# Decode step kernel: a DRAM-to-DRAM copy issued later, and page loads in another order

## The chip, the cores and the metric

The program runs on one core of one Trainium2 chip. The time is device microseconds of one execution. Before the change three executions took 1007.67 (the median), 1008.3 and 1002.5 us.

## The reference, cut to what matters

One inference step of two trunk layers. Each layer normalises its input, multiplies it with one wide weight matrix (`h @ w_in`) and feeds three token mixers: a gated linear recurrence (HGRN2), a sparse attention whose keys are chosen by an indexer (top k), and an attention with compressed, selected and windowed keys. 256 prompt tokens are computed beside 8 decoding sequences, each of which has 1024 past tokens in 8 pages of 128 rows. Beside the outputs the step returns new state:

```python
rows = jnp.concatenate([flat(dk_h), dv, ik_h, flat(nck_h), ncv, flat(nsk_h), nsv], axis=-1)
full = rows if past_rows is None else jnp.concatenate([past_rows.astype(dt), rows], axis=1)
dots = jnp.einsum('bthd,bsd->bths', iqb, ik, ...) * IDX_DIM ** -0.5   # indexer keys of all past tokens
sel = lax.top_k(score, n_top)[1]
wfull = wrows if win_rows is None else jnp.concatenate([win_rows.astype(dt), wrows], axis=1)
return y, rows, wfull[:, -min(WINDOW, lw):], s_new.astype(dt)
```

The third output, for the decoding sequences, is the window state: 511 old rows of each sequence and one new one. The 511 old rows are copied as they are.

## The kernel before, in words

All engines run their own instruction list; they meet at semaphores. Everything is float32. TensorE (PE) sets the order: for each layer it runs projections (L876, weights in 1 MB "slabs"), indexer scores (`key_scores`, L943), the recurrence (L1002 to L1087), prompt attention (L1098 to L1132), the compression of prompt tokens (L1145 to L1192), the page stage of the decoding sequences (L1200 to L1231), decode softmax and values (L1249 to L1311), branch products (L1328) and the output projection (L1336). Between dependent steps it runs pieces of independent projections (`mix`, L992), so that it need not wait.

**Slabs.** `STREAM` is the list of weight slabs in the order of use. There are three slots in SBUF (`NSLOT = 3`); SyncE (SP) loads each slab with `send(name)` (L641), which first waits until the slab three places earlier in the list has been used. The gate slabs g00 to g21 are used in the recurrence, two jobs of 16 matmuls each; m00 to m23 hold the merge gates, two `mix` pieces each.

**Indexer and recurrence.** `key_scores(pair)` waits for indexer keys of a pair of sequences (64 pages of 32 KB per layer; those of even page number are issued by SP, those of odd number by GpSimd, POOL). VectorE (DVE) meanwhile picks the top keys of the prompt (`top_keys`, L1786), and then prepares the factors of the recurrence: step `m i` (L1966, L1967, mark `m 0` at L1968). TensorE's products of step i (L1020, mark `a i`) wait for `m i`; behind each stand two projection jobs at most. Ahead of them PE waits for `sidx_a "relu"` (ScalarE, L1473), runs L1007 (mark `flat`), and DVE merges the products (L1862). SP loads the recurrent state S (2 MB, L693) after `flat`.

**Old window rows.** POOL issues the copy `s_win <- state_win` (L768, 4088 KB read from and written to DRAM) right behind the new rows of the layer (L765, L766). Its landing is waited for at the very end only (L815).

**Page stage.** The 64 key pages are worked in 8 units `u`. `load_keys(u)` brings 8 key pages of 256 KB (128 x 512 float32), 4 on SP (even pages) and 4 on POOL (odd), 2.10 MB together, into one of four buffers `KB[u % 4]`. Units 4 to 7 wait until unit u - 4 has been used (`pg_p`). `load_values(s)` brings 8 value pages of 128 KB (128 x 256 float32), again half on SP and half on POOL, 1.05 MB together. `window_keys(p)` brings 0.52 MB on SP. Unit u on PE is `page_scores` (L1200), for odd u `window_scores` (L1208), `compress` (L1221), and `compressed` (L1229, L1231) behind even ones. PE waits for the keys just ahead of L1200 and for the window keys ahead of L1208. The buffer `KB[3]` lies on memory that the compression stage of the prompt still uses. That stage has the marks `s` (L1158), `t` (L1167), `o` (L1175), `nb` (ScalarE, L1577) and last `sums` (DVE, L2097), which releases unit 3's buffer. Values of all sequences are needed at L1299 only.

SP's and POOL's lists are quoted below: each issues in order, so that a wait in one holds up all that stands behind it.

Of the kernel before, what the change touches and what calls it, by code (L numbers as in the profile page):

```python
# [307 lines left out]
def hybrid_step(nc, x_cols, pages_kv, page_table, state_win, win_k, win_v, state_hgrn, weights, small_w, cmp_w1,  # L308
                const, gate_rows, y_cols, z_keys, z_vals, p_hgrn, s_win, s_hgrn):
    ctx = ExitStack()  # L310
    with ctx:
# [3 lines left out]
        def sem(name):  # L315
            return ctx.enter_context(nc.semaphore(name))
# [204 lines left out]
        hg_p = Steps("hg_p", ["a diag"] + [f"a {i}" for i in range(8)] + ["o", "kfT", "kd", "sfin", "qk", "od", "kv 0", "odT", "kv 1", "ss"])  # L521
# [3 lines left out]
        spill_out, back_in = sem("spill_out"), sem("back_in")  # L525
# [7 lines left out]
        cp_p = Steps("cp_p", ["h", "out", "s", "t", "o"] + [f"gb {c}" for c in range(3)])  # L533
        cp_v = Steps("cp_v", ["sum", "s", "n", "nb", "ev"] + [f"gb {c}" for c in range(3)]
                     + ["sums"])
        cp_a = Steps("cp_a", ["hb", "hid", "out", "e", "nb", "t", "ev"])
# [52 lines left out]
        def page_of(part, l, page):  # L589
            o, rows, cols = PAGE_PARTS[part]  # L590
            return pages_kv[bass.ds(l, 1), bass.ds(page, 1), o:o + rows * cols].rearrange("a b (p c) -> p (a b) c", p=rows)[:, 0]
# [6 lines left out]
                        engine.dma_start(ikT[halves[h], pair, i * PAGE:(i + 1) * PAGE], page_of("index", l, pages[2 * pair + h, i]))\  # L598
                            .then_inc(ik_in[pair][i % 2], 16)

        def load_keys(engine, l, u, odd, pages):

            if u >= 4:
                engine.wait_ge(pg_p.sem, pg_p(l, f"u {u - 4}"))
            for e in range(2):
                for k in (odd, 2 + odd):
                    engine.dma_start(KB[u % 4][:, e, k, :], page_of("keys", l, pages[u // 2 + NPAIR * e, 4 * (u % 2) + k])).then_inc(page_in[u % 4][odd], 16)  # L607

        def load_values(engine, l, s, odd, pages):

            for i in range(odd, NPG, 2):
                engine.dma_start(V[:, s, i, :, :].rearrange("p a c -> p (a c)"), page_of("vals", l, pages[s, i])).then_inc(v_in[odd], 16)  # L612

        def window_keys(engine, l, p):

            if p >= 2:
                engine.wait_ge(pg_p.sem, pg_p(l, f"u {2 * p - 3}"))
            for e in range(2):
                engine.dma_start(kws[p % 2][:, e, :], win_k[l, p + NPAIR * e]).then_inc(win_in[p % 2], 16)
# [11 lines left out]
        def _(sp):  # L631
# [6 lines left out]
            for l in range(DEPTH):  # L638
                l1 = bass.ds(l, 1)

                def send(name):  # L641
                    slot = SLOT_AT[name][0]
                    at_ = STREAM.index(name)
                    if l and at_ < NSLOT:

                        sp.wait_ge(ga_p.sem, ga_p(l - 1, LAST_USE[LAST_IN_SLOT[slot]]))
                    if at_ >= NSLOT:

                        old = STREAM[at_ - NSLOT]
                        if old in SLAB_OF:  # L650
                            sp.wait_ge(proj_ready, l * NJOB + LAST_JOB[old])
                        elif old[0] == "m":
                            sp.wait_ge(mx_p.sem, mx_p(l, LAST_USE[old]))
                        else:
                            sp.wait_ge(ga_p.sem, ga_p(l, LAST_USE[old]))
                    for i, (dst, src) in enumerate(slab_sources(name, l)):
                        if name == "iq0" and i < 2:
                            sp.dma_start(dst, src).then_inc(iq_in[i], 16)
                            if l == 0:
                                x_columns(2 * i + 1)  # L660
                            if l == 0 and i == 0:
                                x_columns(2)
                        else:
                            sp.dma_start(dst, src).then_inc(slab_in[slot], 16)

                for name in FRONT:
# [4 lines left out]
                    if l == 0 and name == "iq1":  # L672
                        sp.dma_start(cst[:, NFIRST:], const[:, NFIRST:]).then_inc(consts_in, 16)
                        sp.dma_start(pt[:, :], page_table.rearrange("(o a) b -> o (a b)", o=1)).then_inc(pages_in, 16)
                        pages = {}
# [40 lines left out]
                sp.wait_ge(cp_p.sem, cp_p(l, "s"))  # L716
                load_keys(sp, l, 2, 0, pages)
                load_values(sp, l, 1, 0, pages)
                sp.wait_ge(cp_v.sem, cp_v(l, "sums"))
                load_keys(sp, l, 3, 0, pages)  # L720
                load_values(sp, l, 2, 0, pages)
                for name in ("m21", "m22"):
                    send(name)
                for u in range(4, NUNIT):
                    load_keys(sp, l, u, 0, pages)
                    if u % 2:
                        window_keys(sp, l, u // 2)
                sp.wait_ge(pg_p.sem, pg_p(l, "u 4"))
                for s in (4, 5):
                    load_values(sp, l, s, 0, pages)  # L730
# [20 lines left out]
        def _(pool):  # L751
# [4 lines left out]
            pages = page_numbers(pool, 1)  # L756
            for l in range(DEPTH):
# [7 lines left out]
                pool.dma_start(z_keys[l], Z[:, Z_IK:Z_IW, :]).then_inc(rows_out, 16)  # L765
                pool.dma_start(z_vals[l], Z[:, Z_NWV:Z_NSV + 1, :]).then_inc(rows_out, 16)  # L766

                pool.dma_start(s_win[l1].rearrange("a s w c -> (a s) w c"),  # L768
                               state_win[l1, :, 1:WIN, :].rearrange("a s w c -> (a s) w c")).then_inc(win_out, 16)

# [23 lines left out]
                pool.wait_ge(cp_p.sem, cp_p(l, "s"))  # L794
                load_keys(pool, l, 2, 1, pages)
                load_values(pool, l, 1, 1, pages)
                pool.wait_ge(cp_v.sem, cp_v(l, "sums"))
                load_keys(pool, l, 3, 1, pages)
                pool.wait_ge(spill_out, l * 16 + 16)
                load_values(pool, l, 2, 1, pages)  # L800
                for u in range(4, NUNIT):
                    load_keys(pool, l, u, 1, pages)
                pool.wait_ge(pg_p.sem, pg_p(l, "u 4"))
# [1484 lines left out]
```

## Time and profile before

| | |
|---|---|
| runs (us) | 1002.5, 1007.67, 1008.3 |
| profiled execution | 1005.99 us, span 1004.3 us, mean granted clock 0.98 |
| PE busy | 956.5 us (95%) |
| DVE busy | 481.1 us (48%) |
| ACT busy | 303.3 us (30%) |
| POOL busy | 132.4 us (13%) |
| DMA | 188.96 MB, mean 188 GB/s |

All times within the execution are counted from the start of the span. Layer 0 lasts to about 505 us, layer 1 to the end, and each stage lies some 495 us later in the second layer. PE, DVE, ACT and POOL are the compute engines.
### The profile page before, as it was taken

The numbers are of one execution on the slowest core, as the hardware profiler recorded it, in microseconds if no ns is written. First come the engines' busy times: TensorE is split into PE (matmuls) and PEld (weight loads), VectorE is DVE, ScalarE is ACT, GpSimd is POOL, SyncE is SP. The second block draws the span as 40 slices with busy tenths as digits, with TensorE's granted clock in tenths as the row PEclk, the third lists the DMA queues.
The fourth block names the chain that finished last, engine by engine and source line by source line (L and its number), as shares of the span: only waits on it lengthen the run. The fifth ranks groups of instructions, "written<-read, shape, count | busy, mean of one in ns | idle before, by whom it ended". The sixth has DMA issues, their size and how long they took to land.

```text
span 1004.3 us, 16669 instructions
## 1 busy us (share of the span) xinstructions
PE 956.5 (95%) x6058; PEld 775.0 (77%) x6058; DVE 481.1 (48%) x1350; ACT 303.3 (30%) x657; POOL 132.4 (13%) x258
## 2 busy tenths in 40 slices
PE   8999989999999979999999999899999997989998
PEld 6888768877777767888888886688676866778887
DVE  4223588877746303124240345898785562041331
ACT  2135413237633112320111463222576311133000
POOL 0510000002031442000060000000020404500000
PEclk9999999999999989999999999999999999899999
DMA  7544635344197797334454446352443949952432
GB/s 256 200 170 153 211 152 210 106 156 169 42 314 264 289 379 255 136 126 136 158 175 139 151 138 261 141 197 85 148 158 100 374 168 380 374 190 87 161 133 86
DMA packets 56212, 188.96 MB, mean 188 GB/s; under 512 B 9154, under 2 KB 22850, under 8 KB 43586
## 3 DMA queue, kind: packets, MB, share of 16 engines
q1 hardware_dynamic: 42850, 138.56, 39.5%
q0 software_dynamic: 12992, 49.16, 12.9%
q8 instruction: 48, 0.79, 0.3%
q14 instruction: 34, 0.28, 0.1%
q10 hardware_dynamic: 288, 0.18, 0.1%
HBM read 177.47 MB, written 18.77 MB: 195 GB/s over the span
## 4 chain that ended last, share of the span: by engine, by line
PE 80%; DMA 7%; DVE 5%; ACT 3%; issue 2%; DVEq 2%; SPq 2%; ACTq 1%
PE ps L876 23%; PE ps L992 16%; PE ps L1328 9%; DMA arena<-in_pages_kv_dram 6%; PE ps L1336 6%; PE ps L1221 4%; PE ps L1020 3%; PE ps L865 2%; PE ps L1299 2%; PE ps L1132 2%; PE ps L1120 2%; PE ps L1100 1%; PE ps L1200 1%; PE ps L903 1%; PE ps L888 1%
## 5 line engine op out<-in xcount | busy, mean ns | idle before, releaser
L876 PE MATMUL ps<-hT,slab 128*128 128x264 f32 (+1 forms) x1184 | 272.8, 389 | 0.0
L876 PEld LDWEIGHTS ps<-hT,slab 128*128 128x128 f32 (+1 forms) x1184 | 224.4, 191 | 39.9 <-issue 2.1
L992 PE MATMUL ps<-hT,slab 128*128 128x264 f32 x768 | 182.9, 395 | 1.7 <-DVEq L2085 1.7
L992 PEld LDWEIGHTS ps<-hT,slab 128*128 128x128 f32 x768 | 145.6, 193 | 34.1 <-issue 3.3
L1348 ACT ACTIVATE arena<-ps 128x512 f32<-128x512 f32 (+21 forms) x152 | 69.7, 484 | 194.4 <-PE ps L876 70.1
L1328 PE MATMUL ps<-Y,slab 128*128 128x264 f32 x384 | 85.8, 386 | 0.0
L1328 PEld LDWEIGHTS ps<-Y,slab 128*128 128x128 f32 x384 | 73.0, 190 | 12.5
L1221 PEld LDWEIGHTS ps<-arena,w 128*128 128x128 f32 x512 | 61.1, 199 | 11.7 <-issue 10.0
L1221 PE MATMUL ps<-arena,w 128*128 128x128 f32 x512 | 64.1, 285 | 0.0
L1740 DVE SCALAR_TENSOR_TENSOR arena<-arena,small 128x264 f32<-128x264 f32 x26 | 11.0, 490 | 110.7 <-ACT arena L1423 110.7
L1336 PE MATMUL ps<-arena,slab 128*128 128x264 f32 x256 | 57.5, 387 | 2.3 <-DVEq L2225 2.3
L1336 PEld LDWEIGHTS ps<-arena,slab 128*128 128x128 f32 x256 | 48.5, 190 | 11.3 <-DVEq L2225 3.1
L598 POOL DMA_DIRECT2D arena<-in_pages_kv_dram x64 | 33.3, 520 | 160.6 <-DVEq L2241 122.5
L607 POOL DMA_DIRECT2D arena<-in_pages_kv_dram x64 | 35.0, 547 | 105.6 <-DVEq L2097 54.6
L2107 DVE TENSOR_TENSOR arena<-ps,arena 64x252 f32<-64x252 f32 x8 | 3.3, 412 | 90.0 <-ACT arena L1348 90.0
L1533 ACT ACTIVATE arena<-arena,st 128x128 f32<-128x128 f32 (+1 forms) x96 | 42.3, 443 | 8.1 <-DVEq L2010 7.1
L1486 ACT ACTIVATE arena<-ps 128x264 f32<-128x264 f32 x38 | 14.8, 389 | 80.5 <-PE ps L992 80.2
L612 POOL DMA_DIRECT2D arena<-in_pages_kv_dram x64 | 35.0, 546 | 29.2 <-PE ps L1221 26.7
L1348 ACT ACTIVATE Y<-ps 128x264 f32<-128x264 f32 x24 | 9.4, 390 | 87.0 <-PE ps L876 87.0
L1200 PE MATMUL ps<-arena,QC 128*32 128x512 f32 x128 | 18.8, 661 | 14.0 <-DMA arena<-in_pages_kv_dram 12.8
L888 PEld LDWEIGHTS ps<-slab,hT 128*128 128x128 f32 x128 | 25.2, 200 | 8.2 <-issue 4.7
L865 PE MATMUL ps<-arena,slab 128*128 128x264 f32 x128 | 30.2, 394 | 0.2 <-issue 0.2
(360 smaller groups left out, 1196.6 us busy)
## 6 DMA issues: line engine op xcount, KB each, us to landing
slab<-in_weights_dram SPq DMA_DIRECT2D x86, 1024.0 KB, 4.9
arena<-in_pages_kv_dram SPq DMA_DIRECT2D x64, 256.0 KB, 11.3
arena<-in_pages_kv_dram POOLq DMA_DIRECT2D x64, 256.0 KB, 8.2
arena<-in_pages_kv_dram POOLq DMA_DIRECT2D x64, 128.0 KB, 6.2
arena<-in_pages_kv_dram SPq DMA_DIRECT2D x64, 128.0 KB, 8.7
out_dram<-in_state_win_dram POOLq DMA_DIRECT2D x2, 4088.0 KB, 27.8
arena<-in_state_hgrn_dram SPq DMA_DIRECT2D x2, 2048.0 KB, 10.1
out_dram<-arena POOLq DMA_DIRECT2D x2, 2048.0 KB, 7.5
```

What stands on the lines that cost most here:

```text
L598: engine.dma_start(ikT[halves[h], pair, i * PAGE:(i + 1) * PAGE], page_of("index", l, pages[2 * pair + h, i]))\
L607: engine.dma_start(KB[u % 4][:, e, k, :], page_of("keys", l, pages[u // 2 + NPAIR * e, 4 * (u % 2) + k])).then_inc(page_in[u % 4][odd], 16)
L612: engine.dma_start(V[:, s, i, :, :].rearrange("p a c -> p (a c)"), page_of("vals", l, pages[s, i])).then_inc(v_in[odd], 16)
L865: last = mm(ps[:, n, 0:LT], stationary(name, job, k), XG[:, k, :], start=(k == 0), stop=(k == KD - 1))
L876: last = mm(ps[0:job[3], n % 2, 0:LT], v[:, k, job[2]:job[2] + job[3]], hT[:, k, :], start=(k == 0), stop=(k == KD - 1))
L888: last = mm(ps[:, n % 2, t * 256:t * 256 + width], hT[:, k, t * 128:t * 128 + 128], v[:, k, o:o + width], start=(k == 0), stop=(k == KD - 1))
L992: last = mm(ps[:, bank, 0:LT], v[:, k, (d % 2) * 128:(d % 2) * 128 + 128], hT[:, k, :], start=(k == 0), stop=(k == KD - 1))
L1221: last = mm(out[:, kv, :, 64 * hf:64 * hf + 64], w1[:, kv, t, :], blocks[:, :, o:o + 2 * NPB8], start=(t == 0), stop=(t == ST - 1))
L1328: last = mm(ps[:, d % 4, 0:LT], v[:, j, dd * 128:dd * 128 + 128], Y[:, a, j, :], start=(j == 0), stop=(j == 3))
L1336: last = mm(ps[:, d % 4, 0:LT], v[:, k, (d % 2) * 128:(d % 2) * 128 + 128], mT[:, k, :], start=(k == 0), stop=(k == KD - 1))
L1348: return A(out, in_, ACT.Copy, scale=scale)
L1533: A(x[:, j, :], x[:, j, :], ACT.Exp, scale=-1.0, bias=st[:, c + j:c + j + 1], accum_out=sa[:, c + j:c + j + 1])
```

## The change

Three edits, each in both layers. POOL waits for `a 0` of the recurrence before it issues the copy of old window rows. Unit 3's keys are loaded in two halves: sequence 0 of each pair after the mark `o`, sequence 1 after `sums`. The values of sequence 2 are issued after `nb`, ahead of the keys of unit 3, and slab m21 is sent between the halves; slab m22 is sent behind the last keys and window keys. POOL's wait for the spill transfer moves up with the values.

```diff
-        def load_keys(engine, l, u, odd, pages):
+        def load_keys(engine, l, u, odd, pages, sequences=(0, 1)):
...
-            for e in range(2):
+            for e in sequences:
...
                 sp.wait_ge(cp_p.sem, cp_p(l, "s"))
                 load_keys(sp, l, 2, 0, pages)
                 load_values(sp, l, 1, 0, pages)
+                sp.wait_ge(cp_a.sem, cp_a(l, "nb"))
+                load_values(sp, l, 2, 0, pages)
+                sp.wait_ge(cp_p.sem, cp_p(l, "o"))
+                load_keys(sp, l, 3, 0, pages, (0,))
+                send("m21")
                 sp.wait_ge(cp_v.sem, cp_v(l, "sums"))
-                load_keys(sp, l, 3, 0, pages)
-                load_values(sp, l, 2, 0, pages)
-                for name in ("m21", "m22"):
-                    send(name)
+                load_keys(sp, l, 3, 0, pages, (1,))
                 for u in range(4, NUNIT):
                     load_keys(sp, l, u, 0, pages)
                     if u % 2:
                         window_keys(sp, l, u // 2)
+                send("m22")
...
+                pool.wait_ge(hg_p.sem, hg_p(l, "a 0"))
                 pool.dma_start(s_win[l1].rearrange("a s w c -> (a s) w c"),
                                state_win[l1, :, 1:WIN, :].rearrange("a s w c -> (a s) w c")).then_inc(win_out, 16)
...
+                pool.wait_ge(spill_out, l * 16 + 16)
+                pool.wait_ge(cp_a.sem, cp_a(l, "nb"))
+                load_values(pool, l, 2, 1, pages)
+                pool.wait_ge(cp_p.sem, cp_p(l, "o"))
+                load_keys(pool, l, 3, 1, pages, (0,))
                 pool.wait_ge(cp_v.sem, cp_v(l, "sums"))
-                load_keys(pool, l, 3, 1, pages)
-                pool.wait_ge(spill_out, l * 16 + 16)
-                load_values(pool, l, 2, 1, pages)
+                load_keys(pool, l, 3, 1, pages, (1,))
```

## Rows read from the trace of the kernel before

**Rows 1.** Waits of PE: line, releaser, us in total, times, longest.
```profile
PE ps L1200 <- DMA arena<-in_pages_kv_dram: 12.8, 2, 7.3
PE ps L943 <- DMA arena<-in_pages_kv_dram: 6.8, 2, 4.1
```

**Rows 2.** Timeline of PE, page stage, layer 0: start, us, operation, [idle before].
```profile
347.83 1.06 PE L1200 MATMUL ps<-arena,QC 128*32 128x512 f32 x8
...
349.25 3.84 PE L1221 MATMUL ps<-arena,w 128*128 128x128 f32 x32
358.67 1.93 PE L1200 MATMUL ps<-arena,QC 128*32 128x512 f32 x8 [5.58 <-DMA arena<-in_pages_kv_dram]
360.54 4.74 PE L1221 MATMUL ps<-arena,w 128*128 128x128 f32 x32
```

**Rows 3.** The same, page stage of layer 1.
```profile
855.14 1.93 PE L1200 MATMUL ps<-arena,QC 128*32 128x512 f32 x8 [7.27 <-DMA arena<-in_pages_kv_dram]
857.01 5.63 PE L1221 MATMUL ps<-arena,w 128*128 128x128 f32 x32
```

**Rows 4.** Stretch behind the wait: us, PE busy, granted clock, DMA share, GB/s.
```profile
358.70:362.30 3.60, 3.60 (x16) 0.50 1.02 381
```

**Rows 5.** The chain that ended last: start, us, what.
```profile
155.93 1.98 PE ps L1020 x16
...
189.99 3.56 PE ps L876 x16
...
339.22 19.40 DMA arena<-in_pages_kv_dram
```

**Rows 6.** Timeline of SP's queue, transfers issued: start, us for all.
```profile
166.85 51.97 SPq L664 DMA_DIRECT2D slab<-in_weights_dram  x6
...
330.95 1.84 SPq L607 DMA_DIRECT2D arena<-in_pages_kv_dram  x4
...
337.33 8.29 SPq L607 DMA_DIRECT2D arena<-in_pages_kv_dram  x8
```

**Rows 7.** DMA queues, 318 to 331 us: packets, MB, share of 16 engines.
```profile
q1 hardware_dynamic: 132, 0.11, 2.7%
```

**Rows 8.** DMA queues, 331 to 373 us.
```profile
q1 hardware_dynamic: 4401, 8.98, 58.9%
```

**Rows 9.** DMA queues, 351 to 360 us.
```profile
q0 software_dynamic: 679, 2.21, 64.4%
q1 hardware_dynamic: 696, 1.27, 39.0%
```

**Rows 10.** DMA queues, 363 to 369 us.
```profile
q1 hardware_dynamic: 1268, 2.31, 104.7%
```

**Rows 11.** Timeline of PE, indexer and first recurrence step; one of layer 0, two of layer 1.
```profile
140.86 1.98 PE L943 MATMUL ps<-arena 128*64 128x512 f32 x4 [4.09 <-DMA arena<-in_pages_kv_dram]
...
635.21 1.72 PE L943 MATMUL ps<-arena 128*64 128x512 f32 x4 [2.73 <-DMA arena<-in_pages_kv_dram]
...
650.64 2.05 PE L1020 MATMUL ps<-arena 128*128 128x128 f32 x16 [0.15 <-DVEq L1968]
```

**Rows 12.** Timeline of DVE, layer 0: last wait ahead of the top keys, end of `m 0`.
```profile
123.58 1.61 DVE L1783 SCALAR_TENSOR_TENSOR arena<-arena 128x128 f32<-128x128 f32 x4 [4.81 <-ACT arena L1454]
...
154.08 0.67 DVE L1967 TENSOR_TENSOR arena<-arena 128x512 f32<-128x512 f32 x1
```

**Rows 13.** Timeline of ACT, layer 0: the mark `relu`.
```profile
153.38 0.59 ACT L1473 ACTIVATE arena<-ps 128x512 f32<-128x512 f32 x1
```

**Rows 14.** Issues of DMA, whole run: count, KB each, median us to landing.
```profile
out_dram<-in_state_win_dram POOLq DMA_DIRECT2D x2, 4088.0 KB, 27.8
```

**Rows 15.** Issues of DMA, window from 111.5 to 113.2 us, same columns.
```profile
slab<-in_weights_dram SPq DMA_DIRECT2D x1, 1024.0 KB, 26.4
```

**Rows 16.** DMA queues, 116 to 139 us.
```profile
q0 software_dynamic: 64, 3.66, 37.2%
q1 hardware_dynamic: 1258, 1.44, 21.9%
```

## The prediction

> **What bounds the kernel now.** The table of busy time comes first: PE has work for 956.5 of 1004.3 us, so only PE's 48 idle us, and the stretches in which its work is slowed, can be won. The waits of PE say which idle time depends on a transfer: 12.8 us ahead of the page scores and 6.8 us ahead of the indexer scores, one wait of each kind in each layer [rows 1]. All other waits are for DVE or ACT and this change does not touch them. Then the timeline of PE around these waits. In the page stage unit 3 ends at 353.09 us (358.67 less 5.58), and unit 4 starts 5.58 us later; in layer 1 it is 7.27 us [rows 2, 3]. Behind the wait the same instructions are slower: the page scores take 1.93 us where they took 1.06, the compression 4.74 (5.63 in layer 1) where it took 3.84. The granted clock of that stretch is 0.50, the lower of PE's two levels, 1.2 GHz [rows 4]; PE had been idle ahead of it. The chain of waits confirms that the end hangs on it: 19.40 us of it are one transfer issued at 339.22, a key page of unit 4 [rows 5].
>
> **Page stage: what is taken away.** Per layer the wait and what follows it: 5.58 + 0.87 (scores) + 0.90 (compression) = 7.35 us in layer 0, 7.27 + 0.87 + 1.79 = 9.93 us in layer 1; together 17.3 us, the most that this part can give.
>
> Why unit 4 was late: SP's queue. Ahead of its four key pages it held, from 330.95 us on, unit 3's half (1.05 MB), half of the values of sequence 2 (0.52) and two slabs (2.10), and with its own 1.05 that makes 4.72 MB, by the sizes in the code [rows 6]. SP's queue moves 1.27 MB in 9 us while POOL's is busy too (0.141 MB/us, POOL's 0.246), and 2.31 MB in 6 us alone (0.385) [rows 9, 10]. After the change only 0.52 MB of unit 3 stands ahead of unit 4.
>
> Where it goes: the first half of unit 3, the values of sequence 2 and slab m21, 3.15 MB in all, now load between 318 and 331 us, where SP's queue moved 0.11 MB [rows 7]. At 0.385 MB/us that is 8 us of an idle stretch, so I cost it at nothing. If that cover were gone, each us by which they overrun 331 us would come off unit 4's 6 us in hand. On SP's list m21's wait (for the slab three places earlier, whose last piece runs just before the mark `o`) stands ahead of unit 3's second half; it is met by then. m22's wait now stands behind all keys and ahead of the values, which are needed 50 us later. The extra waits for `nb` and `o` hold up nothing but what the change itself puts behind them; unit 3's second half and everything later were held by `sums` anyway.
>
> What is late next: I follow SP's queue, with 2 us from issue to first data and 1.7 us from last data to PE (estimates; together they place unit 4's old arrival within 3 us of 358.6). Units take about 5.4 us on PE (347.83 to 353.09 is 5.26, every second one carries a little more), so without waits units 4 to 7 start at 353.1, 358.5, 363.9 and 369.3. Unit 4, issued at 337.3: while POOL moves its half (1.05 / 0.246 = 4.3 us) SP moves 0.6 MB, then 0.45 alone in 1.2 us; there at 346.5, with 6.6 us in hand. Unit 5 is there at 352.6, window keys 2 at 356, unit 6 at 361.6 (2.3 in hand), unit 7 at 367.6 (1.7). The last window keys come behind unit 7 while POOL already loads values: 368.4 to 369.6, plus 1.7, is 370.1 to 371.3 against a need at 370.3. That margin is nought. I take 0.5 us of wait a layer for it, bounds 0 and 3 us. **Page stage: 17.3 - 1.0 = 16.3 us gained.**
>
> **The copy.** Before, it ran under the indexer stage: 27.8 us from issue to landing [rows 14], and a slab issued 2 us after it took 26.4 us to land [rows 15]. Indexer keys issued behind that slab came late, hence PE's waits of 4.09 and 2.73 us [rows 11]. With the copy away these waits should go. But what do they cost? DVE runs from 123.58 us without waiting for anybody until `m 0` ends at 154.75 us [rows 12], and PE's first recurrence product needs it; PE started that at 155.93 us [rows 5]. So in layer 0 PE can gain 1.1 us and no more, and in layer 1, where PE waited 0.15 us for DVE at this very place [rows 11], nothing but that: 0.1. Also ACT's `relu` ends at 153.97 us [rows 13], and it depends on DVE, not on the keys. The time won in the indexer scores is given back as one wait of some 4 us ahead of the recurrence, in each layer. That wait is as long as the one which led to the lower clock in [rows 11] (1.98 and 1.72 us for scores of the same shape as others of 1.08), and now the slow stretch falls on the recurrence, where PE has no time in hand. Price of one such fall, from [rows 2]: 0.87 + 0.90 = 1.8 us. Layer 0: 1.8 - 1.1 = 0.7 slower; layer 1: 1.8 - 0.1 = 1.7 slower. **Indexer stage: 2.4 us lost;** bounds: 1.2 gained if the clock holds, 3.6 lost if none of the lead remains.
>
> In its new place, from 158 us, the copy runs against SP's slabs. Slab g11 is sent at 166.85 us [rows 6] and needed at 189.99 [rows 5], 23.1 us later. With the copy issued at 158 and landing 27.8 us later, at 185.8, what is left of S goes first (issued near 154.5 us, 1.3 MB of its 2.1 have moved when the copy's data start, the rest fits beside it by [rows 16]) and g11 has moved a few packets; its rest takes 1.05 / 0.385 = 2.7 us at most, plus 1.7: 190.2, against a need of 190.7 with the loss above. In layer 1 S's transfer ends before the copy starts, and there is a little more room. I take nothing; bounds nothing and 3.3 us plus a clock fall per layer (if g11 takes 26.4 us as the slab of [rows 15] did). S itself is needed 50 us after its issue. POOL's wait for `a 0` has behind it only the recurrent state's output, due at 215 us: nothing.
>
> **Sum.** The profiled execution is 1005.99 us, its span 1004.3; the median of the runs is 1.7 us higher. 1005.99 - 16.3 + 2.4 = 992.1 us.
>
> **Rivals.**
> (A) *The wait moves to the last keys.* SP's queue stays the slower one, since POOL now runs further ahead and issues values earlier. Window keys 3 then come 3 us late and the clock falls once more: 3 + 1.8 a layer, 9.6 in place of the 1.0 reckoned. For it: the nought margin above. Against: unit 7 has some hand, and SP's queue gets 0.385 MB/us whenever POOL pauses [rows 10]. Time: 992.1 + 8.6 = 1000.7.
> (B) *The copy stalls the recurrence.* g11 lands 26.4 us after its issue in both layers: 3.3 + 1.8 a layer, 10.2: 1002.3. For it: [rows 15]. Against: there the copy came ahead of the slab by 2 us, here by 9.
> (C) *The indexer waits are worth their face value*, if PE's jobs and DVE's both move up: 6.8 + 2 x 1.8 = 10.4 gained in place of 2.4 lost, 979.3. Against it speak [rows 12] and the 0.15 us in [rows 11].
> (D) *Slower: packet for packet.* SP's queue gets one of its small packets for each big one of POOL's. In [rows 9] the two moved 696 and 679 packets but 1.27 and 2.21 MB. If POOL's queue never paused, SP's 5.25 MB of keys 4 to 7 and window keys 2 and 3 would take 5.25 / 0.141 = 37.2 us from 339.3, and be there at 378.2, 7.8 us after the need: 7.8 + 1.8 = 9.6 a layer takes back all of the page stage (+1.9 net). Under the copy SP's queue moved 1.44 MB in 23 us against 3.66 [rows 16], so S and g11 (3.15 MB) would be 1.7 MB short at 185.8; g11 there at 191.9, 1.2 us late plus 1.8, 6.0 in both layers. 1005.99 + 1.9 + 6.0 + 2.4 = 1016.3. It decides when SP's queue gets under 5.25 MB in the 29.3 us up to 368.6, which is 0.18 MB/us; before it had 8.98 MB in 42 us, 0.21 [rows 8], because POOL's queue pauses between units. So the trace of before is on the other side, narrowly.
> The Trainium skill, page "DMA: Bandwidth & Descriptors", section "Queues, rings and completion order", says that each DMA engine takes whole packets in turn from the queues that have work; this speaks for rival D, and the trace agrees with it in [rows 9] as to packets; by that rule alone, with POOL's queue never empty, the time would be that of rival D.
>
> **Chances.** Forecast (gain 10.5 to 18) 0.62; A 0.14; B 0.09; C 0.06; D 0.04; nothing moves (the wait has another cause) 0.05. A measurement of this kernel tells about 1% (10 us) from no change. Faster by more: forecast, C and a third of A and B, 0.76. Within 1%: the rest of A and B and the last case, 0.20. Slower: 0.04. The range takes the best sum of the bounds (17.3 + 1.2 gained: 987.5) and 3.5 us for the spread that the runs show, 984, and reaches to rivals A and B at 1002.
>
> **What would show it.** Page stage: no idle time ahead of L1200 in unit 4, both layers, and no slow L1221 there; unit 7's L1208 is where a wait would stand. Indexer: no wait for DMA at L943, but a wait of about 4 us at L1007 or L1020 for ACT or DVE, with a low clock behind it, and DVE's `m 0` where it was. Copy: issued near 158 us, g11 used at about 190.7 with no DMA wait ahead of it. The prediction is wrong if DVE's chain moves, if the clock stays up, or if units 5 to 7 wait.

## The result, and the profile after

The changed kernel takes 993.34 us (median of 4 executions, 992.16 to 994.63) against 1007.25 (4 executions, 1002.5 to 1008.3): a ratio of 0.9856, 95% interval 0.9822 to 0.9890, so 14 us faster. The forecast was 992.1. Beside each of the three groups of experiments below the kernel before ran again; its medians there are 1005.61, 1005.71 and 1005.62 us, and the ratios given with the experiments refer to these. Its profiled execution took 992.23 us, with a span of 990.6 and a granted clock of 0.986.

The page stage first. The timeline of PE in layer 0 at unit 4, which answers to [rows 2]: start, us, operation, idle time before in brackets.

```profile
352.66 1.07 PE L1207 MATMUL ps<-arena,QC 128*32 128x512 f32 x8
353.66 3.84 PE L1228 MATMUL ps<-arena,w 128*128 128x128 f32 x32
```

The wait is gone and the scores and the compression run at their full speed (1.07 and 3.84 us, where they took 1.93 and 4.74). In layer 1 the wait ahead of unit 4 is gone as well, but the last window keys are late; the same view, unit 7:

```profile
857.19 1.07 PE L1207 MATMUL ps<-arena,QC 128*32 128x512 f32 x8
860.82 0.64 PE L1215 MATMUL ps<-arena,QC 128*32 128x256 f32 x8 [2.57 <-DMA arena<-in_win_k_dram]
```

The issues of DMA around these window keys, layer 0 and then layer 1: count, KB each, median us to landing. They were issued from 354.76 and from 843.04 us, so in layer 0 they were there at 367 to 368, some 2 us ahead of their use at 369.87.

```profile
arena<-in_win_k_dram SPq DMA_DIRECT2D x2, 256.0 KB, 11.6
...
arena<-in_win_k_dram SPq DMA_DIRECT2D x2, 256.0 KB, 13.7
```

What moved into the idle stretch: SP's queue from 318 to 331 us, which answers to [rows 7].

```profile
q1 hardware_dynamic: 1874, 3.13, 66.1%
```

It carried 0.11 MB there before, and 3.13 now. Of the 3.15 MB that the change moves up, only 2.10 are on SP's queue (half of the keys, half of the values, the slab); the rest is on POOL's. That 3.13 comes close to 3.15 is chance: part of it is what SP's queue had moved before 318 us in the kernel before. From 290 to 331 us it moved 7.00 MB before and 9.31 now.

Now the indexer stage and the start of the recurrence. All waits of PE that are new (line, releaser, us in total, times, longest):

```profile
PE ps L1014 <- ACT arena L1480: 8.7, 2, 4.4
...
PE ps L1215 <- DMA arena<-in_win_k_dram: 2.6, 1, 2.6
```

The waits for indexer keys of [rows 1] are not in the list any more. In their place PE waits for ScalarE's relu, once in each layer. The timeline of PE in layer 0, which answers to [rows 11], and a stretch of it with its granted clock (us, PE busy, granted clock, DMA share, GB/s):

```profile
147.38 2.05 PE L1009 MATMUL ps<-arena 128*128 128x128 f32 x16
153.69 1.04 PE L1014 MATMUL ps<-arena 64*8 64x256 f32 x8 [4.26 <-ACT arena L1480]
154.66 3.78 PE L1027 MATMUL ps<-arena 128*128 128x128 f32 x16
158.23 4.56 PE L883 MATMUL ps<-hT,slab 128*128 128x264 f32 x16
162.62 1.95 PE L1027 MATMUL ps<-arena 128*128 128x128 f32 x16
```
```profile
154.20:161.00 6.80, 6.80 (x33) 0.58 0.80 292
```

PE is through with L1009 at 149.4 us, waits 4.26 us for L1014, and starts the recurrence at 154.66 us, 1.3 us earlier than in [rows 5]. Then it runs at the lower clock and reaches the second product at 162.62, where the timeline of before has it at 161.31. From the first product to the second it takes 7.96 us; before it took 5.45. VectorE's first factor ended where it had ended, as the timeline of DVE shows (answers to [rows 12]; 153.68 + 0.68 is 154.36, before it was 154.75):

```profile
153.68 0.68 DVE L1974 TENSOR_TENSOR arena<-arena 128x512 f32<-128x512 f32 x1
```

The copy itself was issued by POOL at 158.73 us. The issues of DMA at 158 to 159.5 us and at 166 to 169 us (slab g11, issued at 168.17), and g11's first use:

```profile
out_dram<-in_state_win_dram POOLq DMA_DIRECT2D x1, 4088.0 KB, 25.4
...
slab<-in_weights_dram SPq DMA_DIRECT2D x1, 1024.0 KB, 16.9
```
```profile
191.14 3.73 PE L883 MATMUL ps<-hT,slab 128*128 128x264 f32 x16
```

The slab was slow (16.9 us, the median slab 4.9) and landed at 185.1 us, 6 us ahead of its use.

The stages of all profiled executions, read as the distance of starts in the timeline of PE, in us, layer 0 / layer 1. "Indexer" is from the first indexer product of the prompt to the second recurrence product, "recurrence and attention" from there to the prompt compression, "compression" from there to unit 0, "pages" from unit 0 to the products behind unit 7 (L1254 before), "values" from there to the first branch product. Between the layers lie 176.65 us in all of them; ahead of the first stage the kernels differ by less than 1 us.

| kernel | profiled us | indexer | recurrence, attention | compression | pages | values |
|---|---|---|---|---|---|---|
| before | 1005.99 | 48.4 / 47.5 | 122.4 / 122.4 | 48.6 / 48.6 | 51.5 / 54.1 | 48.2 / 47.8 |
| after | 992.23 | 50.0 / 50.0 | 122.4 / 122.4 | 47.0 / 47.0 | 44.1 / 46.9 | 48.2 / 48.2 |
| after, again | 998.68 | 50.4 / 50.6 | 122.4 / 122.4 | 51.6 / 48.6 | 44.1 / 44.1 | 49.8 / 48.2 |
| pages only | 986.77 | 48.2 / 47.5 | 122.4 / 122.4 | 48.6 / 47.0 | 44.1 / 44.1 | 48.2 / 48.1 |
| copy only | 1014.29 | 48.7 / 48.6 | 122.4 / 122.4 | 48.6 / 52.0 | 54.4 / 54.5 | 48.2 / 48.2 |
| before, no copy | 1010.10 | 49.0 / 50.1 | 122.4 / 122.4 | 51.6 / 47.0 | 52.2 / 53.0 | 48.2 / 47.9 |
| wait filled | 986.57 | 47.7 / 46.0 | 122.4 / 122.4 | 50.0 / 47.0 | 46.3 / 44.1 | 46.5 / 48.1 |
| job up | 987.57 | 47.4 / 47.5 | 119.3 / 119.5 | 47.0 / 51.6 | 45.3 / 44.1 | 49.9 / 49.8 |
| job up, old copy | 993.09 | 53.3 / 50.9 | 118.8 / 118.8 | 47.0 / 51.6 | 44.1 / 44.1 | 48.2 / 49.8 |
| job up, window keys on POOL | 979.92 | 45.7 / 47.5 | 119.2 / 119.6 | 48.6 / 48.6 | 44.1 / 44.1 | 48.2 / 48.2 |
| m22 late only | 1003.05 | 49.6 / 47.4 | 122.4 / 122.4 | 46.9 / 50.1 | 50.7 / 48.7 | 48.2 / 49.8 |
| early loads, m22 as before | 987.70 | 49.1 / 47.3 | 122.4 / 122.4 | 47.0 / 48.6 | 44.1 / 44.1 | 48.1 / 48.2 |

Before against after, in both layers together: pages 14.6 us less, compression 3.4 less, indexer 4.1 more, values 0.4 more. That makes 13.5 of the 13.7 us by which the spans differ.

### The profile page after: what moved, and what is told of

It is laid out like the page before. It is cut to its first block, busy times and chain, and to the rows that moved or that the text cites. A ratio compares the mean times of both kernels' runs of the same rounds, so it can differ in the third digit from the quotient of the medians.

```text
span 990.6 us, 16671 instructions
## 1 busy us (share of the span) xinstructions
PE 952.4 (96%) x6058; PEld 775.3 (78%) x6058; DVE 480.5 (49%) x1350; ACT 303.4 (31%) x657; POOL 132.4 (13%) x258
## 4 chain that ended last, share of the span: by engine, by line
PE 83%; DVE 6%; ACT 4%; DVEq 2%; DMA 2%; issue 2%; ACTq 1%; SPq 1%
PE ps L883 24%; PE ps L999 16%; PE ps L1335 9%; PE ps L1343 6%; PE ps L1228 5%; PE ps L1027 3%; PE ps L872 2%; PE ps L1306 2%; DMA arena<-in_win_k_dram 2%; PE ps L1139 2%; PE ps L1127 2%; PE ps L1207 1%; DVE top L1796 1%; PE ps L1107 1%; DVEq L1799 1%
## 5 line engine op out<-in xcount | busy, mean ns | idle before, releaser
L999 PE MATMUL ps<-hT,slab 128*128 128x264 f32 x768 | 179.6, 391 | 1.7 <-DVEq L2092 1.7
L1228 PEld LDWEIGHTS ps<-arena,w 128*128 128x128 f32 x512 | 58.4, 192 | 10.0 <-issue 6.6
L1228 PE MATMUL ps<-arena,w 128*128 128x128 f32 x512 | 61.4, 279 | 0.0
L1343 PEld LDWEIGHTS ps<-arena,slab 128*128 128x128 f32 x256 | 48.6, 191 | 11.1 <-DVEq L2232 3.1
L1027 PEld LDWEIGHTS ps<-arena 128*128 128x128 f32 x224 | 30.3, 212 | 2.5 <-DVEq L1975 1.7
L1027 PE MATMUL ps<-arena 128*128 128x128 f32 x224 | 30.9, 298 | 0.0
```

The lines of the kernel that those rows point to most:

```text
L999: last = mm(ps[:, bank, 0:LT], v[:, k, (d % 2) * 128:(d % 2) * 128 + 128], hT[:, k, :], start=(k == 0), stop=(k == KD - 1))
L1027: last = mm(ps[:, b + t, h * 128:h * 128 + 128], x, x, start=True, stop=True)
L1228: last = mm(out[:, kv, :, 64 * hf:64 * hf + 64], w1[:, kv, t, :], blocks[:, :, o:o + 2 * NPB8], start=(t == 0), stop=(t == ST - 1))
L1343: last = mm(ps[:, d % 4, 0:LT], v[:, k, (d % 2) * 128:(d % 2) * 128 + 128], mT[:, k, :], start=(k == 0), stop=(k == KD - 1))
```

## The experiments

The theory: the page edits give all of the gain, through what stands ahead of unit 4 in SP's queue; the move of the copy gives nothing, since VectorE and not the keys sets the start of the recurrence, and costs the lower clock behind the new wait. The rival: the waits for indexer keys were worth what they lasted, 7 us and a lower clock on top.

**Page edits alone.** The copy stays where it was.

```diff
-                pool.wait_ge(hg_p.sem, hg_p(l, "a 0"))
                 pool.dma_start(s_win[l1]...
```

> The page stage as in the changed kernel, the copy of old window rows where it was. Theory (the page stage gives everything, the moved copy costs because VectorE sets the start of the recurrence): gain of 14 to 15 us in the page stages kept (44 us and 47 us from unit 0 to the scores), PE's waits of 4.1 and 2.7 us for indexer keys back, no wait for ScalarE ahead of the recurrence, and the whole 3 to 4 us faster than the changed kernel: 988 to 991 us. Rival (the moved copy pays its face value of 10 us): about 1002 us. If the prompt compression behind attention is again at full clock, the 3 us won there have to do with the page edits or with chance; if it is slow again in both layers, with the copy's place.

Measured: 991.34 us (6 executions, 986.77 to 997.37), ratio to the kernel before 0.9867 (0.9834 to 0.9900). The timeline of PE, layer 0:

```profile
140.35 1.97 PE L949 MATMUL ps<-arena 128*64 128x512 f32 x4 [3.88 <-DMA arena<-in_pages_kv_dram]
142.25 7.79 PE L894 MATMUL ps<-slab,hT 128*128 128x256 f32 x32
...
154.82 0.61 PE L1013 MATMUL ps<-arena 64*8 64x256 f32 x8
155.37 2.05 PE L1026 MATMUL ps<-arena 128*128 128x128 f32 x16
```

The wait for keys is back, the one ahead of the recurrence is not, and the recurrence starts only 0.7 us later than in the changed kernel, at full clock. The two page stages, with their granted clock:

```profile
331.81:375.92 44.11, 42.85 (x379) 1.00 0.94 345
817.51:861.61 44.10, 42.84 (x378) 1.00 0.95 346
```

44.1 us in both layers: 17.4 us less than before, all that was to be had. The median is a little above the expected 988 to 991 us, and the profiled execution below. The rival (1002 us) is out. The compression was slow in one layer and fast in the other, so its time hangs neither on the copy nor on the page edits.

**The changed kernel again**, on the same chip.

> The changed kernel itself on the same chip, to compare the others with: 992 to 995 us. A second profile shows whether the full clock in the prompt compression (1.5 us a layer faster than before) and the wait for window keys 3 in layer 1 alone are properties of the kernel or chance.

Measured: 994.07 us (6 executions, 989.45 to 998.68), ratio 0.9869 (0.9835 to 0.9902), the profiled execution 998.68. No wait for window keys in either layer this time (pages 44.1 / 44.1). In the compression PE, idle for 0.86 us only, worked a stretch at the lower clock; timeline, and stretches with the granted clock:

```profile
321.06 6.78 PE L999 MATMUL ps<-hT,slab 128*128 128x264 f32 x16 [0.86 <-DVEq L2092]
```
```profile
321.50:328.30 6.80, 6.80 (x24) 0.59 1.02 375
328.30:332.00 3.70, 3.70 (x20) 1.00 0.09 37
```

Products of the same form and number take 3.83 us right behind them. So both the compression's 3 us and the late window keys come and go between executions of one kernel. By total time this kernel and the one with the page edits alone (2.7 us less by medians) can't be told apart, since their intervals cover each other; by the indexer stage they can: 100.0 and 101.0 us for both layers in the two profiles of this one, where the four profiles with the copy in its old place and no other edit in that stage have 95.7 to 97.1.

The same timeline shows that the stage holds a second slow stretch, which comes without any copy too (4.77 us in layer 1 of the kernel that leaves it out):

```profile
117.37 6.24 PE L883 MATMUL ps<-hT,slab 128*128 128x264 f32 x16
...
156.21 3.62 PE L1027 MATMUL ps<-arena 128*128 128x128 f32 x16 [0.15 <-DVEq L1975]
...
163.29 1.95 PE L1027 MATMUL ps<-arena 128*128 128x128 f32 x16
```

The projection ahead of VectorE's top keys took 6.24 us here and 4.69 in the first profile of this kernel; in the two shortest indexer stages of the table (46.0 and 45.7) it took 3.83. VectorE began the top keys 1.75 us later for it (125.02 against 123.27), so the bound itself moved. Behind the new wait, on the other hand, the clock cost less: 7.08 us from the first recurrence product to the second, in both layers, and not 7.96 and 7.87.

**The copy's move alone.**

```diff
+                pool.wait_ge(hg_p.sem, hg_p(l, "a 0"))
                 pool.dma_start(s_win[l1]...
```

> Only the copy moved into the recurrence, the page loads as before. Theory: no wait for indexer keys, a wait of 4.3 us for ScalarE ahead of the recurrence in both layers and a low clock behind it, 3.7 us slower than before in those stretches: 1009 to 1011 us if nothing else moves, 1006 to 1008 if the prompt compression wins its 3 us here. Rival (indexer waits are worth 10 us): 996 us. Rival (copy stalls a gate slab): a wait for a slab in the recurrence.

Measured: 1007.22 us (12 executions, 1004.84 to 1014.29), ratio 1.0017 (0.9996 to 1.0039): no gain, and the 10 us of the rival are excluded. Waits of PE:

```profile
PE ps L1201 <- DMA arena<-in_pages_kv_dram: 17.0, 2, 8.8
PE ps L1008 <- ACT arena L1474: 8.7, 2, 4.4
```

The wait for ScalarE is the one of the changed kernel, to a tenth. No slab was waited for. The median is below the 1009 to 1011 us that were expected if nothing else moves. The expected 3.7 us more in these stretches came only in part: the indexer stage takes 1.4 us more than before in this profile, where the changed kernel's took 4.1. From the first recurrence product to the second it is 6.78 and 6.39 us, so how much the lower clock takes differs by execution. The wait for unit 4 is longer here, 8.2 and 8.8 us in the two layers against 5.6 and 7.3, with the page loads untouched; in the kernel without a copy it is 6.2 and 6.1. So it varies by some 3 us with these loads as they are, and the reason is open.

**Before, without the copy.** The old window rows are not written at all, the rest is as before.

```diff
-                pool.dma_start(s_win[l1].rearrange("a s w c -> (a s) w c"),
-                               state_win[l1, :, 1:WIN, :].rearrange("a s w c -> (a s) w c")).then_inc(win_out, 16)
...
-            pool.wait_ge(win_out, DEPTH * 16)
```

> The kernel before without the copy of old window rows (that output is left unwritten): 8 MB of DRAM reads and as many of writes less. Theory (VectorE's chain from 123.6 us to the first recurrence factor is the bound, PE only changes where it waits): no gain, about 1006 to 1010 us, the indexer wait replaced by one of 4.3 us for ScalarE and a low clock behind it. Rival (the contention costs what the waits say): 996 us.

Measured: one execution, 1010.1 us, against a median of 1005.61 for the kernel before. Timeline of PE, layer 0:

```profile
153.93 0.62 PE L1004 MATMUL ps<-arena 64*8 64x256 f32 x8 [4.26 <-ACT arena L1470]
154.69 3.64 PE L1017 MATMUL ps<-arena 128*128 128x128 f32 x16
```

Leaving out 8 MB of copy wins nothing in the indexer stage: 99.1 us in both layers against 95.9. PE reaches its bound earlier, waits there, and pays with the clock. One execution can't settle the total, but the stage is plain.

**The wait filled.** Eleven idle products in the changed kernel's hole.

```diff
+                for _ in range(11):
+                    mm(ps[:, 4, 0:LT], ident, hT[:, 0, :], start=True, stop=True)
                 pe.wait_ge(sidx_a.sem, sidx_a(l, "relu"))
```

> The changed kernel with 11 idle products of 264 columns (0.39 us each, 4.2 us in all, into a bank that is overwritten next) ahead of the wait for ScalarE's relu: the wait is filled, the start of the recurrence is not moved. Theory (the moved copy costs because the wait lowers the clock and the slow stretch falls on the recurrence): no idle time and no low clock there, first to second recurrence step in 5.4 us in both layers and not in 7 to 8, 3 to 5 us off the time: 989 to 991 us. Rival (the step is slow for another reason, a slab under the copy): first to second step stays at 7 us or more, time as the changed kernel, 993 to 995.

Measured: 987.97 us (4 executions, 986.57 to 993.25), ratio 0.9839 (0.9808 to 0.9870). Timeline of PE, layer 0:

```profile
149.16 5.06 PE L1012 MATMUL ps<-hT,cst 128*128 128x264 f32 x22
154.15 0.61 PE L1016 MATMUL ps<-arena 64*8 64x256 f32 x8
154.70 2.05 PE L1029 MATMUL ps<-arena 128*128 128x128 f32 x16
...
160.15 1.95 PE L1029 MATMUL ps<-arena 128*128 128x128 f32 x16
```

First to second product: 5.45 us in both layers, as before the change, and not 7.96 and 7.87 (or 7.08). The start at 154.70 is that of the changed kernel's first profile (154.66), the granted clock of the stretch from 154.2 to 161 us is 1.00 here and 0.58 there, and the copy still runs under the recurrence (issued at 157.05 us; the slab behind it took 19.2 us to land). So the price of the moved copy is the clock, 1.6 to 2.5 us a layer in the changed kernel's two profiles, and no slab. The median is 1 us below the expected range; the intervals of this kernel and the changed one (0.9835 to 0.9902) overlap, so that the stage shows it and not the total.

**Work in the hole.** One gate job is taken from behind the eighth recurrence step and put ahead of the first; ScalarE's relu goes ahead of its first exponential.

```diff
                 last.then_inc(sidx_p.sem, sidx_p.mark("flat"))
+                project(*next(gates))
                 for i in range(8):
...
                     project(*next(gates))
-                project(*next(gates))
...
-                act.wait_ge(hg_v.sem, hg_v(l, "d 0"))
-                A(E_, E_, ACT.Exp).then_inc(hg_a.sem, hg_a.mark("e 0"))
                 evacuate("hi1", 0)
                 act.wait_ge(skey_p.sem, skey_p(l, "dot 3"))
                 A(RI, ps[:, 6, :], ACT.Relu).then_inc(sidx_a.sem, sidx_a.mark("relu"))
                 evacuate("hi1", 1)
+                act.wait_ge(hg_v.sem, hg_v(l, "d 0"))
+                A(E_, E_, ACT.Exp).then_inc(hg_a.sem, hg_a.mark("e 0"))
```

> The changed kernel with one gate projection job (16 matmuls, 3.56 us) run ahead of the first recurrence step and one less behind the eighth; ScalarE's evacuation of hi1 and its relu stand ahead of its first exponential, so that PE's wait goes from relu to VectorE's first factor. Theory (with the copy moved, PE has 4.3 us idle here in each layer that can hold real work): 3.56 us less in both layers and little or no low clock: 10 us less than the changed kernel, 983 to 986 us. Rival (VectorE's chain is the bound through the whole recurrence): the job taken from the end is missing there and PE waits for VectorE behind the eighth step, no gain, 990 to 994.

Measured: 986.14 us (6 executions, 980.97 to 989.57), ratio 0.9792 (0.9762 to 0.9822). Timeline of PE, layer 0, and two of the waits of PE:

```profile
149.92 3.83 PE L883 MATMUL ps<-hT,slab 128*128 128x264 f32 x16
154.50 2.05 PE L1028 MATMUL ps<-arena 128*128 128x128 f32 x16 [0.75 <-DVEq L1975]
...
159.95 1.95 PE L1028 MATMUL ps<-arena 128*128 128x128 f32 x16
```
```profile
PE ps L1028 <- DVEq L1975: 1.6, 2, 0.9
...
PE ps L883 <- DMA slab<-in_weights_dram: 0.4, 1, 0.4
```

The real job stands where PE was idle, the clock holds, and behind the eighth step nothing is missing: indexer, recurrence and attention take 166.7 and 167.0 us together where the changed kernel has 172.4 in both, 11 us in all. Of these the medians show 8, and this profile had low-clock stretches in the later stages; with the idle products it was 338.4 for both layers, so that some 6 of the 11 us were to be had by filling the wait alone, and the intervals of the two kernels overlap. The median is just above the expected range. PE now waits 0.75 us for VectorE ahead of the first product (0.9 in layer 1), so a second job could win no more than that.

The wait for a slab is new. With the job moved up a slot comes free earlier: in layer 1 a gate slab is issued at 645.67 us, 3.3 us behind the copy (642.37), takes 23.5 us to land and is 0.44 us late. In the changed kernel the first slab behind the copy was issued 9 us after it and was there in time.

**The same, with the copy in its old place.**

```diff
-                pool.wait_ge(hg_p.sem, hg_p(l, "a 0"))
```

> The same with the copy of old window rows back in its first place. Theory: here PE is held 4 and 2.7 us by late indexer keys and has no idle time ahead of the recurrence; the job moved up delays the first step, and nothing is won by it: 990 to 992 us, as the kernel with the page edits alone, 6 to 8 us slower than the one with the copy moved. So the copy's move would be worth its face value only together with work to put into the hole. Rival (the place of the copy makes no difference): as the kernel with the copy moved.

Measured: 992.21 us (6 executions, 988.35 to 994.98), ratio 0.9857 (0.9832 to 0.9882). Waits of PE:

```profile
PE ps L949 <- DMA arena<-in_pages_kv_dram: 7.3, 2, 4.4
```

The interval is wholly above that of the kernel with the copy moved. In layer 0 the first recurrence product starts 5.5 us later than with the page edits alone (160.85 against 155.37), and the loop then saves 3.6. So the move of the copy is worth 6 us of 1000 beside the job moved up, and nothing that the totals show without it (994.07 against 991.34).

**Window keys 1 and 3 on POOL**, added to the job moved up.

```diff
-                window_keys(sp, l, 1)
...
-                    if u % 2:
-                        window_keys(sp, l, u // 2)
+                    if u == 5:
+                        window_keys(sp, l, 2)
...
+                pool.wait_ge(spill_out, l * 16 + 16)
+                window_keys(pool, l, 1)
...
+                window_keys(pool, l, 3)
```

> The kernel with the job moved up and the copy in the recurrence, and window keys of pairs 1 and 3 issued by POOL instead of SP. Theory (window keys 3 are the last item of SP's queue and arrive with no margin; the one wait of 2.6 us in layer 1 of the changed kernel was that): no wait ahead of L1208's counterpart in any layer, time as without this edit or up to 2 us less: 982 to 986 us. Rival (POOL's longer list delays values or keys): a wait at the keys of unit 4 to 7 or at the values.

Measured: 980.4 us (5 executions, 979.92 to 983.59), ratio 0.9759 (0.9736 to 0.9782), the best of all and 2.4% below the kernel before, a little below the expected range. No wait for keys, window keys or values is in its profile, but one of 0.6 us for a gate slab under the copy, which took 23.7 us to land. From the page:

```profile
PE 948.3 (97%) x6058; PEld 770.1 (79%) x6058; DVE 480.6 (49%) x1350; ACT 306.0 (31%) x657; POOL 137.1 (14%) x266
```

Whether this last edit wins anything is open: the intervals with and without it overlap, and the wait that it is to prevent is small and not always there: 2.6, 2.0 (filled wait, layer 0) and 1.0 us (job up, layer 0) in three of the eight page stages profiled with the changed kernel's page loads and the copy moved, none in the other five.

**Slab m22 alone moved.**

```diff
-                for name in ("m21", "m22"):
-                    send(name)
+                send("m21")
                 for u in range(4, NUNIT):
...
+                send("m22")
```

> The kernel before with slab m22 alone moved behind the last keys (the copy, unit 3 and the values of sequence 2 as before). Theory (unit 4's keys are late by what stands ahead of them in SP's queue): 1.05 MB less there, at 0.385 MB/us alone and 0.27 beside POOL's keys some 2.7 to 4 us earlier, so that the wait ahead of unit 4 falls from 5.6 and 7.3 us to 1 to 4 us; page stages 46 to 51 us each in place of 51.5 and 54.1. Rival (the wait is for POOL's half or for bandwidth as a whole, whose total up to the last key is cut by 1 MB in 15): no less than 4.5 and 6 us.

Measured: one execution, 1003.05 us; pages 50.7 / 48.7. Timeline of PE: unit 4 in layer 0, then units 4 and 5 in layer 1.

```profile
357.38 1.94 PE L1200 MATMUL ps<-arena,QC 128*32 128x512 f32 x8 [4.48 <-DMA arena<-in_pages_kv_dram]
...
849.18 1.06 PE L1200 MATMUL ps<-arena,QC 128*32 128x512 f32 x8 [0.91 <-DMA arena<-in_pages_kv_dram]
...
858.11 0.64 PE L1208 MATMUL ps<-arena,QC 128*32 128x256 f32 x8 [1.82 <-DMA arena<-in_win_k_dram]
```

Layer 1 is as expected (7.27 down to 0.91 ahead of unit 4, though unit 5, its window keys and unit 6 then wait 0.4, 1.8 and 1.0), layer 0 is not (5.58 to 4.48, a little above the expected range). The rival wanted no less than 4.5 and 6 us; it all but holds in one layer and falls in the other. In the three profiles with the page loads of before unit 4 waits 5.6 to 8.8 us, so both waits here are below all of those. One megabyte is thus too little, and how late unit 4 comes varies by some us between layers and executions.

**Early loads, m22 as before.** The page edits with m22 ahead of unit 4, the copy in its old place.

```diff
                 load_keys(sp, l, 3, 0, pages, (1,))
+                send("m22")
...
-                send("m22")
```

> The kernel with the page edits alone (copy in its first place), but slab m22 right behind unit 3's second half and ahead of unit 4, as before the change. Theory: the 3.15 MB moved into the idle stretch ahead of the mark sums are enough; unit 4's keys come 2.7 us later than with m22 behind them but still ahead of the need by 3 us, so no wait ahead of unit 4 and page stages of 44.1 us, or a short one at a later unit. Rival (every MB counts and m22's place is needed): a wait of 2 us or more ahead of unit 4.

Measured: one execution, 987.7 us. Pages 44.1 / 44.1, and unit 4 in layer 0 without a wait and at full speed:

```profile
351.98 1.07 PE L1206 MATMUL ps<-arena,QC 128*32 128x512 f32 x8
352.98 3.84 PE L1227 MATMUL ps<-arena,w 128*128 128x128 f32 x32
```

The 3.15 MB that moved into the idle stretch (2.10 of them on SP's queue) are enough; m22's new place was not needed in this execution.

## Why the prediction was right

**Page stage, forecast 16.3 us less, measured 14.6** in the changed kernel's profile and 17.4 in its second one and in that with the page edits alone. Both waits of [rows 2, 3] and the slow products behind them are gone. That the loads ahead of unit 4 were the cause is shown: the early loads alone remove the wait, a single slab less on SP's queue removes a part. That it was SP's half and not POOL's, whose loads move up as well, the trace of before shows; issues of DMA from 338.7 to 340.3 us:

```profile
arena<-in_pages_kv_dram POOLq DMA_DIRECT2D x3, 256.0 KB, 10.3
arena<-in_pages_kv_dram SPq DMA_DIRECT2D x2, 256.0 KB, 18.3
```

POOL's last keys of unit 4 were issued by 340.1 and so there by about 350.4, ahead of the end of unit 3 (353.09). SP's page issued at 339.22 took 18 us. The margins fell as worked out: units 4 to 7 did not wait for keys, and where a wait came (one of four stages, 2.57 us) it was at window keys 3, whose margin had been put at nought. The 0.5 us a layer taken for it was a fair mean (2.57 and 2.0 in the eight stages of the changed kernel's two profiles, the page edits alone and the filled wait); in the one profile rival A came in one layer of two, with no fall of the clock behind it.

**Indexer stage, forecast 2.4 us lost, measured 4.1.** The mechanism was right: waits for keys gone, a wait of 4.3 and 4.4 us ahead of the recurrence, for ScalarE's relu, VectorE's `m 0` where it was, the clock low behind it. Two terms were off. The clock's price, taken as 1.8 us a layer from the stretch behind unit 4, was 2.5 and 2.4 (7.96 and 7.87 us from the first product to the second, 5.45 with the wait filled); this step stayed at the lower level for most of 6.8 us. The lead, taken as 1.1 and 0.1 us, was 1.0 and -0.1 (from the first indexer product to the first of the recurrence 42.98 and 42.02 us before, 42.02 and 42.12 after). But 2.5 is the price in this execution: in the four profiles that have the new wait the step takes 7.96, 7.87, 7.08, 7.08, 6.78, 6.39, 7.08 and 7.93 us, on the mean 1.8 above 5.45, as had been taken. And the lead can be lost to the slow projection ahead of the top keys, which the prediction did not look at. It says that VectorE runs from 123.58 us without waiting for anybody; there is one wait of 0.26 us for ScalarE, at 125.45. Rival C, the face value of 10 us, is refuted three times: by the changed kernel, by the copy's move alone and by the kernel without a copy.

**The copy in its new place, forecast nothing.** It landed after 25.4 us, at 184.1, g11 one microsecond later, 16.9 us after its issue and 6 us ahead of its use, where I had reckoned half a microsecond. S was through 7.6 us after its issue, and so did not stand ahead of g11 under the copy; that this is the whole reason is argued, not shown. Rival B did not come here. Its mechanism, a slab sent too soon behind the copy, came on a small scale with the job moved up, 0.4 and 0.6 us in one layer.

**Not forecast:** 3.4 us won in the compression. It has nothing to do with the change. The timeline of the first profile of the kernel before (not among the rows ahead) and of the changed kernel, layer 0, the 16 products behind 32 narrow ones (36 columns):

```profile
287.26 5.49 PE L992 MATMUL ps<-hT,slab 128*128 128x264 f32 x16
```
```profile
288.58 3.81 PE L999 MATMUL ps<-hT,slab 128*128 128x264 f32 x16
```

Over all profiles here this stage takes 47.0, 48.6 or 50 to 52 us, in kernels that do not differ there. It hid the other two errors: 1.7 us too much for the page stage and 1.7 too little for the indexer stage went one way, these 3.4 the other, and the profiled execution came out at 992.23 where 992.1 had been worked out. That the total agrees to a tenth of a microsecond is luck; what was right is the size of the page stage and that the copy's move wins nothing. The second series of both kernels has 994.07 against 1005.61, a gain of 11.5 us.

Rival D, packet for packet without a pause, did not come either. From 339.3 to 368.6 us SP's queue moved 5.77 MB in 2850 packets, 0.20 MB/us where the rival needed less than 0.18, and POOL's 5.24 MB in 1661. Two of the prediction's sums are inexact, without bearing on the forecast: the 3.15 MB that it lets SP's queue move between 318 and 331 us are those of both queues, and in rival D the copy's 6.0 us count all of S, of which 1.3 MB had moved by the prediction's own figures; without them the rival would be at 1010.3.

## What to carry to other kernels

A wait in the profile is worth what the next bound leaves of it: before you cost it, follow the other engines to where they meet again. Here 7 us of waits for keys hid behind VectorE, and their removal cost time in the stage until the hole was filled; the copy's move and the job moved up won together what neither did alone. When a buffer's loads come late, read the queue in order of issue: moving 3 MB (2 of them on the late queue) into an idle stretch ahead of them was worth 17 us, and the bandwidth had been there all along.

## What the runs showed of the hardware

The lower clock came without an idle stretch right ahead of it. In the kernel with the page edits alone, PE was busy by the profile for the whole of both stretches below (the last wait ahead of them in its timeline, of 0.57 us, ended at 277.35), and yet the second was granted the lower level for most of it; the changed kernel ran the same products at full clock (us, PE busy, granted clock, DMA share, GB/s):

```profile
282.00:287.00 5.00, 5.00 (x39) 0.99 0.98 358
287.30:290.70 3.40, 3.40 (x10) 0.56 0.98 351
```

What PE had done before it fell were the 32 products of 36 columns; that they are the reason is not shown. The ends of products are modelled in the profile, so that short pauses between them would not be seen. The Trainium skill, page "TensorE: Matmul & The Clock Gate", section "HAM oscillation — how this bites in real kernels", explains such falls by PE's waits for transfers. Behind the new wait ahead of the recurrence the trace agrees as to a wait, though this one is for ScalarE (4.26 us idle, then 0.58 granted); at this stretch it differs, since PE had waited for no transfer, and the measurement decides. Such stretches, of 1.7 or 3 us of loss each, come at the same few places but not in every execution. Between the two profiled executions of the changed kernel, 992.23 and 998.68 us, they make 6.3 us in the compression, 1.6 in the values and 1.0 net in the indexer stage; against them stands the wait for window keys that only the first had. A difference of less than 5 us between two kernels is better read from the stage that was edited than from one pair of totals.

One large copy from DRAM to DRAM slows another queue's slab from 4.9 us (the median of all) to 26.4 [rows 15], 16.9 or, issued 3.3 us behind the copy, 23.5, though it does not fill the DMA engines' time: 37.2% and 21.9% for the two queues [rows 16].
